# Row maxima of the attention exchanged through a DRAM buffer instead of TensorE transpositions

## The reference, cut to what matters

```python
s = jnp.einsum('brhnid,brhnjd->brhnij', qb, kc).astype(jnp.float32) * (Dh ** -0.5)
s = jnp.where(valid, s, -jnp.inf)
m = jnp.max(s, axis=-1, keepdims=True)
p = jnp.exp(s - m)
denom = jnp.sum(p, axis=-1, keepdims=True)
o = jnp.einsum('brhnij,brhnjd->brhnid', p, vc.astype(jnp.float32)) / denom
lse = (m + jnp.log(denom))[..., 0]
...
wts = jax.nn.softmax(jnp.stack(lses, axis=0), axis=0)
o = jnp.sum(wts[..., None] * jnp.stack(outs, axis=0), axis=0)
```

## Time and profile before

| what | value |
|---|---|
| median of 3 runs | 941.86 us (940.86 to 942.62) |
| the profiled execution, its own time | 943.0 us |
| its span in the trace | 941.2 us |
| PE busy | 913.2 us, 97% of the span |
| DVE busy | 526.6 us, 56% |
| ACT busy | 372.7 us, 40% |
| chain that ended last, PE's share | 90% |

### The profile page before, as it was taken

How to read it: one execution, slowest core, us unless ns; L and a number is a source line. 1 busy time by engine, 2 the same in 40 slices (tenths; PEclk the granted TensorE clock), 3 DMA queues, 4 the chain that set the end, 5 groups by cost and what they waited for, 6 DMA issues and landing times.

```text
span 941.2 us, 12174 instructions
## 1 busy us (share of the span) xinstructions
PE 913.2 (97%) x4741; PEld 776.3 (82%) x4741; DVE 526.6 (56%) x686; ACT 372.7 (40%) x461; POOL 35.9 (4%) x33
## 2 busy tenths in 40 slices
PE   3999999999999999999999999999999999999996
PEld 3998788889898888888888788888888888888885
DVE  5868865637664667752444467555555556532223
ACT  6441216593434356343122245333433333422225
POOL 0010000000000000000012120000000000000003
PEclk9899999999999999999999999999999999999998
DMA  9946626115251424252222540343333342223202
GB/s 327 361 155 170 174 62 188 45 46 178 95 175 46 163 107 160 109 179 90 90 90 68 201 135 1 102 114 97 89 89 89 98 112 102 90 96 117 99 0 89
DMA packets 114270, 112.87 MB, mean 120 GB/s; under 512 B 4676, under 2 KB 104390, under 8 KB 111927
## 3 DMA queue, kind: packets, MB, share of 16 engines
q1 hardware_dynamic: 113511, 110.16, 37.3%
q10 hardware_dynamic: 720, 2.16, 0.6%
HBM read 104.77 MB, written 4.19 MB: 116 GB/s over the span
## 4 chain that ended last, share of the span: by engine, by line
PE 90%; DVE 3%; ACT 2%; DMA 2%; SPq 2%; issue 1%; DVEq 0%; ACTq 0%
PE bank L1643 25%; PE bank L1645 24%; PE bank L1644 24%; PE bank L1860 2%; PE bank L1957 1%; PE bank L2113 1%; DMA x<-x_spill 1%; PE bank L1763 1%; PE bank L1801 1%; PE bank L1881 1%; PE bank L1962 1%; PE bank L1758 1%; PE bank L1774 1%; PE bank L1735 1%; PE bank L1927 1%
## 5 line engine op out<-in xcount | busy, mean ns | idle before, releaser
L1643 PE MATMUL bank<-h_hi,w_hi 128*128 128x512 f32 x672 | 267.0, 397 | 1.7 <-ACT sB L852 0.8
L1645 PE MATMUL bank<-h_hi,w_lo 128*128 128x512 f32 x672 | 261.8, 390 | 0.0
L1644 PE MATMUL bank<-h_lo,w_hi 128*128 128x512 f32 x672 | 261.7, 389 | 0.0
L1643 PEld LDWEIGHTS bank<-h_hi,w_hi 128*128 128x128 f32 x672 | 126.3, 188 | 28.5 <-issue 2.1
L1645 PEld LDWEIGHTS bank<-h_hi,w_lo 128*128 128x128 f32 x672 | 126.1, 188 | 26.7
L1644 PEld LDWEIGHTS bank<-h_lo,w_hi 128*128 128x128 f32 x672 | 126.3, 188 | 25.5 <-issue 0.2
L1094 DVE TENSOR_TENSOR w_lo<-raw,w_hi 128x2048 fp32r<-128x2048 f32 (+2 forms) x46 | 85.6, 1871 | 60.7 <-ACT w_hi L598 55.1
L1101 DVE TENSOR_TENSOR w_lo<-raw,w_hi 128x2048 fp32r<-128x2048 f32 x31 | 71.1, 2293 | 86.4 <-ACT w_hi L606 86.4
L1597 DVE SCALAR_TENSOR_TENSOR conv<-bank,vecs,conv 128x511 f32<-128x511 f32 x88 | 65.7, 747 | 65.8 <-ACT conv L986 60.3
L598 ACT ACTIVATE w_hi<-raw 128x2048 fp32r<-128x2048 f32 (+2 forms) x44 | 71.7, 1642 | 49.7 <-DMA raw<-in_w_in_dram 49.7
L606 ACT ACTIVATE w_hi<-raw 128x2048 fp32r<-128x2048 f32 x31 | 59.1, 1905 | 69.3 <-PE bank L1645 69.3
(11 more groups left out here) (269 smaller groups left out, 1326.6 us busy)
## 6 DMA issues: line engine op xcount, KB each, us to landing
raw<-in_w_up_dram SPq DMA_DIRECT2D x44, 512.0 KB, 4.5
raw<-in_w_in_dram SPq DMA_DIRECT2D x19, 1024.0 KB, 5.3
raw<-in_ada_w_dram SPq DMA_DIRECT2D x16, 1024.0 KB, 5.7
raw<-in_w_down_dram SPq DMA_DIRECT2D x22, 512.0 KB, 3.7
raw<-in_w_in_dram SPq DMA_DIRECT2D x20, 512.0 KB, 5.2
ada_in<-in_ada_w_dram SPq DMA_DIRECT2D x16, 512.0 KB, 9.8
raw<-in_w_gla_branch_dram SPq DMA_DIRECT2D x4, 1024.0 KB, 4.9
raw<-in_w_out_dram SPq DMA_DIRECT2D x4, 1024.0 KB, 5.0
```

Of the source, the lines that this page charges most:

```text
L1643: pe.matmul(out_ap, wh, xh, start=first, stop=False, skip_group_check=True)
L1644: pe.matmul(out_ap, wh, xl, start=False, stop=False, skip_group_check=True)
L1645: return pe.matmul(out_ap, wl, xh, start=False, stop=last, skip_group_check=True)
```

## The change

Steps 2 and 3 lose all their TensorE work and the two DVE operations on rows. In their place SP writes the maxima with two DMAs into a DRAM buffer `mx_dram`, laid out by token, the one half from token order and the other from residue order, and reads them back with two DMAs crosswise into `mx_other`, so that each column holds the other groups' maxima in its own order. DVE then takes the maximum of `mx` and `mx_other` and scales it. The runs of consecutive bytes in DRAM are 8 bytes (512 of them) for one half of each direction and 32 bytes (128 of them) for the other. The exchange of p = 0 stands in SP's program ahead of the step that shuffles rotation 4 and loads unit `gqk` of GLA head 0, that of p = 1 ahead of the load of unit `gv` of GLA head 1.

```diff
+        mx_dram = nc.dram_tensor("mx_dram", [2, 2, SEQ, 2], F32, kind="Internal").ap()
...
+            def exchange(p):
+
+                own = mx_dram[p, 0].rearrange("(b l) h -> l b h", b=NB), mx_dram[p, 1].rearrange("(l r) h -> l r h", r=DIL)
+                other = mx_dram[p, 1].rearrange("(b l) h -> l b h", b=NB), mx_dram[p, 0].rearrange("(l r) h -> l r h", r=DIL)
+                sp.wait_ge(mx_done, 2 * p + 2)
+                for half in range(2):
+                    sp.dma_start(own[half], mx[:, half * NB:(half + 1) * NB, :]).then_inc(mx_out, 16)
+                sp.wait_ge(mx_out, 32 * (p + 1))
+                if p > 0:
+                    sp.wait_ge(negm_done, p)
+                for half in range(2):
+                    sp.dma_start(mx_other[:, half * NB:(half + 1) * NB, :], other[half]).then_inc(mx_in, 16)
+
             for q in range(N_RAW):
                 what, n = RAW[q]
+                if what == "w" and n in (UNIT[("gqk", 0, 0)], UNIT[("gv", 1, 0)]):
+                    exchange(0 if n == UNIT[("gqk", 0, 0)] else 1)
                 if what == "w" and 6 <= n < 12:
                     shuffle(n - 6)
...
                     if hd == 0 and bk == 0 and p > 0:
-                        dve.wait_ge(mxr_ps, p)
+                        dve.wait_ge(mx_out, 32 * p)
+                        dve.wait_ge(negm_done, p)
...
-                if i == 2:
-                    dve.wait_ge(mxr_ps, p + 1)
-                    if p > 0:
-                        dve.wait_ge(mxc_ps, p)
-                    dve.tensor_copy(rowm[:, 0, :], side[0][0:2, :]).then_inc(rowmax_done, 1)
-                    dve.wait_ge(rowmax_done, 2 * p + 1)
-                    dve.tensor_tensor(rowm[:, 1, :], side[1][0:2, :], rowm[:, 0, :], ALU.max).then_inc(rowmax_done, 1)
                 if i == 3:
-                    dve.wait_ge(mxc_ps, p + 1)
+                    dve.wait_ge(mx_in, 32 * (p + 1))
+                    dve.tensor_tensor(mx_other[:, :, :], mx_other[:, :, :], mx[:, :, :], ALU.max).then_inc(mx_all, 1)
+                    dve.wait_ge(mx_all, p + 1)
                     if p > 0:
                         dve.wait_ge(exp_done, 8 * p)
-                    dve.tensor_scalar(negm[:, :, :].rearrange("p a b -> p (a b)"), side[0][:, 0:16],
-                                      -DH ** -0.5, None, ALU.mult).then_inc(negm_done, 1)
+                    dve.tensor_scalar(negm[:, :, :], mx_other[:, :, :], -DH ** -0.5, None, ALU.mult).then_inc(negm_done, 1)
...
-                if i == 2:
-                    pe.wait_ge(mx_done, 2 * p + 2)
-                    for b in range(NB):
-                        pe.transpose(side[0][0:2, b * P:(b + 1) * P], mx[:, b, :], ident)
-                    for r in range(DIL):
-                        last = pe.transpose(side[1][0:2, r::DIL], mx[:, NB + r, :], ident)
-                    last.then_inc(mxr_ps, 1)
-                if i == 3:
-                    pe.wait_ge(rowmax_done, 2 * p + 2)
-                    for b in range(NB):
-                        pe.transpose(side[0][:, 2 * b:2 * b + 2], rowm[:, 1, b * P:(b + 1) * P], ident[0:2, 0:2])
-                    for r in range(DIL):
-                        c0 = 2 * (NB + r)
-                        last = pe.transpose(side[0][:, c0:c0 + 2], rowm[:, 1, r::DIL], ident[0:2, 0:2])
-                    last.then_inc(mxc_ps, 1)
```

More of the change, by code:

```diff
@@ L216, in hybrid_block_kernel @@
             ("cs", 108, [P, 2, SEQ], F32))
-        qk, rope, oa_hi, oa_lo, ocomb, osum, orec, oa32, rope_t, v_ext, S, PT, mx, mg, rowm, negm = region(
+        qk, rope, oa_hi, oa_lo, ocomb, osum, orec, oa32, rope_t, v_ext, S, PT, mx, mx_other, mg, negm = region(
             ("qk", 0, [DH, GROUPS, 2, 2, SEQ], F32), ("rope", 24, [P, 2, 2, SEQ], F32),
@@ L223, in hybrid_block_kernel @@
             ("v_ext", 56, [P, NB, GROUPS, HEADS, P], F32), ("S", 80, [P, 2, 1920], F32),
-            ("PT", 95, [P, 1920], F32), ("mx", 102.5, [P, 8, 2], F32), ("mg", 102.75, [P, 2, 4], F32),
-            ("rowm", 103, [2, 2, SEQ], F32), ("negm", 107, [P, 8, 2], F32))
+            ("PT", 95, [P, 1920], F32), ("mx", 102.5, [P, 8, 2], F32), ("mx_other", 102.625, [P, 8, 2], F32),
+            ("mg", 102.75, [P, 2, 4], F32), ("negm", 107, [P, 8, 2], F32))
         q_in, k_in, gv, gr, logs, za, lrT, w2s, og_hi, og_lo, kk, at_sb, kt_sb, ke, state, eb, enb, ed, qB, o_sb, osq, ors = region(
@@ L295, in hybrid_block_kernel @@
         sc_done, msk_done, mx1_done, mx_done = sem("sc_done"), sem("msk_done"), sem("mx1_done"), sem("mx_done")
-        mxr_ps, rowmax_done, mxc_ps, negm_done = (sem(n) for n in ("mxr_ps", "rowmax_done", "mxc_ps", "negm_done"))
+        mx_out, mx_in, mx_all, negm_done = (sem(n) for n in ("mx_out", "mx_in", "mx_all", "negm_done"))
         exp_done, tr_ps, pt_act, pt_dve, pv_done = (sem(n) for n in ("exp_done", "tr_ps", "pt_act", "pt_dve", "pv_done"))
```

## The result

The changed kernel takes 937.22 us (median of 5 runs, 935.78 to 938.23) and the kernel before, beside it, 942.62 (5 runs, 940.86 to 945.52). The ratio is 0.994, with a 95% interval of 0.9918 to 0.9962: faster, by 3.6 to 7.7 us. Two later measurements of the same kernel with more runs on each side gave 938.41 against 941.68 (ratio 0.9963, 0.9948 to 0.9978) and 937.45 against 941.56 (0.9963, 0.9949 to 0.9976): 3.5 us.

A forecast was written before the change was run, and what follows sets the result against it. The prediction took PE to bound the kernel, occupied 478.23 of 480 us around the change. Its terms, 3.39 + 0.24 - 0.1 = 3.5 us, taken from the median of 941.86 gave 938.4 us, range 937.7 to 942.0.

The forecast's parts named there:

- PE's transpositions, 3.6 us: PE at p = 0 and 1: four removed batches give 3.39 us, faster first matmuls behind them 0.24.
- The time h of a pair of DMAs, 2.4 us: Exchange on SP: from a pair's second issue to its landing 2.4 us; up to 3.2 at no cost at p = 0.
- the cover at p = 0: At p = 0 the exchange's reads may land up to 135.6 at no cost; they were expected at 133.95.
- the forecast took off 0.1: At p = 0, 0.1 us lost between PE's transposes (0.15 to spare) and the gqk product (0.2 to spare).
- On SP itself ... no loss.: SP's queue at p = 0: the shuffle issued at 133.43 waits for SP until 132.2, so it loses nothing.
- The late exchange: Rival at p = 0: h between 3.2 and 5.3 us, PE stalls by 2h - 6.4 and the gain shrinks; chance 0.22.
- a stall over 2 us costs about 1.2 more: In the very late exchange rival (chance 0.16): PE's clock falls behind such a stall, costing five matmuls, 1.2 us.
- The few waits of PE further on ... move with it.: PE's later waits, the longest 2.05 us for x1, follow from PE's own releases and so shift without changing the gain.
- The range's low end, 937.7: Fastest time in the forecast's range: no loss at the exchange, and the switches dearer than counted.
- switches dearer than counted: PE's first matmul behind a batch takes 0.31 us where 0.23 is the pace: 0.08 each, 0.24 counted behind three batches.
- the forecast sum: Whole kernel: 3.39 + 0.24 - 0.1 = 3.5 us gained.
- The 4.8 us that the prediction tried for the writes: Rule against the change: short DRAM writes at twice 2.4 us, PE stalls 0.75 at p = 0, time 939.2.

The follow-up runs named there:

- exchange unused: The kernel before with the four exchange DMAs and DVE's waits for them added, result not used: 943.17 against 941.68 us, ratio 1.0016.
- before, again: The kernel before, unedited, profiled and timed a second time: 940.97 against 941.68 us, ratio 0.9998.
- the 32 transpositions: 32 one-element transpositions added at PE's start, in both kernels: before 940.99 against 940.81 us, ratio 1.0000; changed kernel 938.56, ratio 0.9969.

## Why the prediction was wrong in its range and right in its sum

The time came out 0.5 us below the range. Two steps of the prediction failed: the low end of its range, which left no room for the scatter of a median of five, and the late waits of PE, which it put at nothing ("they move with it") and which gave 2.4 us in the first profile. Which of the two put this median outside is not settled, as the last two points say. The terms one by one:

- **PE's transpositions, 3.6 us.** Right, a little small: 1.93 to 1.98 at p = 0 (1.85 forecast) and 1.91 to 1.94 at p = 1 (1.78), shown by the kernel without exchange as well (1.93 and 1.92).
- **The time h of a pair of DMAs, 2.4 us.** Mis-sized: in the first profile the writes took 3.1 us and the reads 3.4, 6.5 together, where the prediction allowed 6.4 at no cost. So the cover at p = 0 was used up and passed by some 0.15 us: PE's transposes took 2.01 us in place of 1.80, and 1.87 and 1.86 in the two later profiles, so 0.2 was lost there in the first and 0.07 in the others (the forecast took off 0.1). That it was no more is partly luck. At p = 1 DVE waited 1.94 us, at no cost, since ACT was still busy:

```profile
181.08 0.17 DVE L1237 TENSOR_TENSOR mx_other<-mx_other,mx 128x16 f32<-128x16 f32 x1 [1.94 <-DMA mx_other<-mx_dram]
...
185.65 3.95 ACT L725 ACTIVATE S<-S,negm 128x256 f32<-128x256 f32 x12
```

- **"On SP itself ... no loss."** Failed in the first profile and held in the others. I had priced the shuffle's issues at 0.6 each; there the eight took 1.5 us more, the load of `gqk` came later, and of the 1.98 gained at p = 0 0.9 was given back: 0.7 at the product of `gqk`, the rest at the transposes. The long issue goes with an instruction fetch, as the last section shows, and not with the short runs of the exchange. In the kernel before, the fetch came at 132.5, while SP had nothing to issue.
- **The late exchange** stayed a rival and was a true one: with the writes doubled, PE waits for the exponentials at the transposes of p = 0 and the gain is gone. The clock fell behind three waits of at most 1.09 us there and behind one of 1.81 (exchange unused), and not behind one of 1.63 (before, again), so the prediction's "a stall over 2 us costs about 1.2 more" was too simple.
- **"The few waits of PE further on ... move with it."** This step failed in the trace. The wait for `x1` shrank from 2.05 and 1.63 us in the two profiles of the kernel before to 0.57 to 0.77 in the three of the changed one, because where instructions are fetched had moved. That explains why the spans differ by 5.1 where the attention gave 1.08 + 1.94 = 3.0 (1.3 from the reload, some 1.1 between there and the end, mostly the clock, less 0.3 of a later start). In the timed runs the share of this is not settled: shifting the fetch alone changed nothing measurable in the kernel before (1.0000, within 0.11%).
- **The range's low end, 937.7.** I let it reach 0.7 below the forecast, for switches dearer than counted, and gave nothing to the scatter of a median of five, though the prediction itself says that a measurement can tell no less than 1.9 us, and as it turned out the start alone scatters by over 3 us between profiles and the median of the kernel before came out at 942.62, 941.68, 941.50, 941.56 and 940.81 in five measurements. With more runs the change is worth 3.5 us (0.9963, twice) and, with the late wait nearly out of both kernels, 3.45: the forecast sum. The 5.4 of the first measurement has 3.6 at the near end of its interval, so that the 1.9 above the sum may be scatter, a gain at the late wait, or both.

## What to carry to other kernels

Moving a small reordering off a saturated engine pays by the gaps it leaves between kept instructions, as long as the detour fits under other work; write down by how much it fits, as here one more round trip of 4 us ate all of it. What stands behind the detour in the issuing queue has less slack than its order suggests. And do not credit a change with what a late, distant wait does in a single profile: profile both kernels more than once, and take that wait out of both before comparing. Where an instruction fetch falls is part of a kernel's timing: when instructions go out of a long stream, the fetches behind them meet other DMAs.

## What the runs showed of the hardware

The writes to DRAM were over on the DMA engines long before SP could go on. In the profile after (window, length, busy of PE, PEld, DVE, ACT, POOL, clock, DMA share, GB/s):

```profile
129.00:130.00 1.00, 1.00 (x6) 0.84 (x5) 1.00 (x2) 0.00 (x0) 0.00 (x0) 1.00 0.97 66
130.00:131.00 1.00, 1.00 (x7) 0.80 (x6) 0.97 (x2) 0.53 (x1) 0.00 (x0) 1.00 0.03 1
131.00:132.00 1.00, 1.00 (x6) 0.84 (x5) 0.53 (x1) 0.00 (x0) 0.00 (x0) 1.00 0.00 0
```

The engines are idle from about 130.1, and the reads are issued at 132.06. So of the 3.2 us nearly 2 lie behind the last packet of the 640 short runs. The Trainium skill (DMA: Bandwidth & Descriptors, Anatomy of one DMA, on DMAs that GpSimd issues) says that the fixed cost is mostly the wait for the write's receipt; the trace of these DMAs, which SP issued, fits that, with 1.9 us here. The 4.8 us that the prediction tried for the writes did not come out.

A 16 KB fetch of instructions at the start of a 2 MB load went with a later landing, in all six of the 16 profiles that had one there (8.7 to 10.3 us, against 7.7 to 8.1 without), and moving the fetch moved the late landing in both kernels. The Trainium skill (Runtime: NRT & Kernel Launch, Instruction fetch mechanics) says that instructions are fetched in blocks of 16 KiB and that this is mostly hidden; the block size agrees, and here no wait of PE is put down to the fetch itself, but the load beside it came late. How one packet does that is open.

The same fetches lengthen SP's issues and the exchange's reads. From 114 to 160 us of the 16 profiles there are eleven issues of 1.16 to 2.10 us, where 0.6 is usual, and at each a packet on q8 starts during it or during the issue just ahead of it; where such a packet came while SP had nothing more to issue, no issue was long. (One of 1.04 us, in the run with the writes twice, has no packet beside it.) The dummy work that shifted the fetches moved the long issues too: the shuffle of the changed kernel went back from 6.43 to 4.95 us, and the kernel before, which has no exchange, got a long issue in an earlier shuffle, with the packet at 126.7 (first row the changed kernel, second row the kernel before, both with the 32 transpositions):

```profile
131.16 4.95 SPq L464 DMA_DIRECT2D qk<-rope  x8
...
126.72 2.10 SPq L463 DMA_DIRECT2D qk<-rope  x1
```

The second read at p = 0 landed after 3.1 to 3.9 us in the six profiles in which a packet on q8 came between the first read's issue and this landing, and after 1.7 to 1.9 in the four in which none did.
